# A hybrid decoder layer: the down projection of its FFN as two passes of Strassen's seven products

## The chip, the cores and the metric

One NeuronCore of a Trainium2 chip runs the whole program. The metric is the device time of one execution in microseconds (us), over several executions. One more execution was recorded by the profiler; its rows are shown below.

## What is computed

One layer in float32 on 512 tokens of width 1024. Three mixers (a conv module, a sparse attention, a Mamba-2 scan) come first. Behind them stands the FFN, which is all that the change touches (D_FF is 2816):

```python
h = rms_norm(x, norm_ffn_g[i])
f = causal_dwconv(h @ w_up[i], ffn_conv_w[i], ffn_conv_b[i])      # 512 x 5632, 3 taps
fa, fg = jnp.split(f, 2, axis=-1)
x = x + (jax.nn.silu(fg) * fa) @ w_down[i]                          # (512 x 2816) @ (2816 x 1024)
```

## The kernel before

Every large product is done in three matmuls: an operand a is split into a high part (a_hi, a copy rounded to the matmul's type, by ScalarE) and a rest (a_lo = a - a_hi, by VectorE), and `product` adds a_hi*b_hi, a_hi*b_lo and a_lo*b_hi in one PSUM bank. A matmul is 128x128 stationary by 128x512 moving.

Weights come in chunks of 1 MB (128 partitions x 2048 floats). A chunk is loaded by SyncE's queue (SP) into one of NSLOT = 2 slots of `w_raw`, in two transfers of 512 KB; ScalarE writes `w_hi`, VectorE `w_lo`; then SP may load the chunk after next into that slot (it waits for `w_lo_ready`), and TensorE may use the chunk. No scheduler is at work in this part: each engine's program is a list in the order of the code, and semaphores join them.

**The up stage.** There are NF = 22 chunks, UP0 to UP0+21; I call them up chunks 0 to 21. Each holds 128 columns of both halves of w_up, and gives two PSUM groups (v = 0, 1) of 24 matmuls. From up chunk 1 on, all engines run loops over rounds of two chunks (s = 0, 1). While TensorE works on a chunk, ScalarE makes `w_hi` of the next, then for each group `f` (the bank times the last tap, plus the bias), then `sg` = silu of the gate. VectorE makes `w_lo` of the next chunk, two more taps on `f` for each group (which frees the bank, semaphores `drained`), `gg` = f*sg, and, once ScalarE has made `g_hi` of it, `g_lo`.

**The down stage.** TensorE takes 11 chunks of w_down (256 rows each) against `g_hi` and `g_lo`. Each chunk is 48 matmuls: 4 blocks of tokens x 2 halves of the columns x 2 blocks of rows x 3. All eight banks accumulate through the whole stage (DOWN_BANK; the four banks of the up stage come last). At the end VectorE adds each bank to x2 into `y_out` (L1495), and SP stores it.

## Time and profile before

| | |
|---|---|
| time, median of 3 runs | 732.29 us (732.28 to 732.38) |
| time of the profiled execution | 732.33 us |
| its span from the first to the last instruction | 730.6 us |
| TensorE busy | 711.4 us, 97% of the span |
| VectorE, ScalarE, GpSimd busy | 459.6, 350.6, 141.9 us |
| granted TensorE clock | 1.00 throughout |
| moved by DMA | 69.48 MB, a mean of 95 GB/s |

The profile is a page of sums and a trace that can be asked for single instructions. Busy is the share of time in which an engine had an instruction at work. A matmul's recorded duration (389 ns) is longer than its share of the time, since matmuls are pipelined: the distance from one start to the next is what counts. A wait is put down to the engine whose signal came last.

### The profile page before, as it was taken

How to read it: one execution, taken by the hardware profiler on the slowest of the kernel's cores; microseconds unless marked ns; L12 is line 12 of the kernel's file. 1: busy time of each engine (PE TensorE's matmuls, PEld its weight loads, DVE VectorE, ACT ScalarE, POOL GpSimd, SP SyncE). 2: the span in 40 equal slices, each digit the busy share in tenths (PEclk: the TensorE clock that was granted, in tenths of full speed). 3: DMA queues.
4: the chain of work that ended last, by engine and by line, in shares of the span. 5: the costliest groups of instructions: out<-in, count | busy, mean ns of one | idle time of the engine just before them, and what ended most of it. 6: DMA issues, size and time to landing. Idle time of an engine off the chain costs nothing.

```text
span 730.6 us, 9609 instructions
## 1 busy us (share of the span) xinstructions
PE 711.4 (97%) x3468; PEld 572.1 (78%) x3468; DVE 459.6 (63%) x703; ACT 350.6 (48%) x532; POOL 141.9 (19%) x114
## 2 busy tenths in 40 slices
PE   4999999899999999999999999999999999999998
PEld 4776888667667788778798888888888888888886
DVE  5368989988998838777666655655656655221223
ACT  6354654989778585532654434434443443122120
POOL 2000569935555203143300000000000000000000
PEclk9999999999999999999999999999999999999999
DMA  9731314123031141212423343243243233322302
GB/s 247 231 116 59 116 59 115 59 79 95 12 103 43 52 195 60 87 58 59 116 58 84 89 115 92 81 115 100 72 115 108 64 115 115 116 66 107 116 1 115
DMA packets 78048, 69.48 MB, mean 95 GB/s; under 512 B 5815, under 2 KB 64535, under 8 KB 78015
## 3 DMA queue, kind: packets, MB, share of 16 engines
q1 hardware_dynamic: 77871, 68.51, 30.7%
q10 hardware_dynamic: 144, 0.52, 0.2%
q8 instruction: 21, 0.34, 0.2%
q14 instruction: 12, 0.10, 0.0%
HBM read 66.91 MB, written 2.12 MB: 94 GB/s over the span
## 4 chain that ended last, share of the span: by engine, by line
PE 86%; ACT 7%; DVE 4%; issue 2%; DMA 1%; POOL 0%; DVEq 0%; ACTq 0%
PE bank L1507 76%; PE bank L1513 3%; PE bank L1527 2%; ACT w_hi L857 1%; ACT tapped L1052 1%; PE bank L1715 1%; DVE u_acc L604 1%; PE bank L1771 1%; PE bank L1691 1%; DVE xbcT L1302 1%; PE bank L1666 1%; DMA x_in<-in_x 1%; ACT prob L975 1%; ACT dec L1022 0%; DVE prob L1281 0%
## 5 line engine op out<-in xcount | busy, mean ns | idle before, releaser
L1507 PE MATMUL bank<-h_hi,w_hi 128*128 128x512 f32 (+1 forms) x496 | 192.9, 389 | 0.0
L1507 PE MATMUL bank<-h_lo,w_hi 128*128 128x512 f32 (+1 forms) x496 | 189.9, 383 | 0.0
L1507 PE MATMUL bank<-h_hi,w_lo 128*128 128x512 f32 (+1 forms) x496 | 189.8, 383 | 0.0
L614 DVE TENSOR_TENSOR w_lo<-w_raw,w_hi 128x2048 fp32r<-128x2048 f32 x34 | 78.5, 2309 | 83.3 <-ACT w_hi L857 83.2
L1507 PEld LDWEIGHTS bank<-h_hi,w_hi 128*128 128x128 f32 x496 | 93.2, 188 | 25.4 <-issue 7.8
L1507 PEld LDWEIGHTS bank<-h_hi,w_lo 128*128 128x128 f32 x496 | 93.2, 188 | 18.6
L1507 PEld LDWEIGHTS bank<-h_lo,w_hi 128*128 128x128 f32 x496 | 93.3, 188 | 17.3
L857 ACT ACTIVATE w_hi<-w_raw 128x2048 fp32r<-128x2048 f32 x34 | 65.0, 1911 | 80.3 <-PE bank L1507 77.8
L783 POOL TENSOR_TENSOR u_acc<-tapped,u_acc 128x511 f32<-128x511 f32 (+29 forms) x60 | 90.1, 1502 | 46.1 <-ACT tapped L1052 43.0
L1468 DVE SCALAR_TENSOR_TENSOR f<-bank,prm,f 128x511 f32<-128x511 f32 x88 | 65.8, 748 | 51.3 <-ACT f L1102 44.9
L1102 ACT ACTIVATE f<-bank,prm 128x512 f32<-128x512 f32 x44 | 33.9, 770 | 95.3 <-PE bank L1507 95.3
L1507 PE MATMUL bank<-w_hi,g_hi 128*128 128x512 f32 x176 | 68.5, 389 | 0.0
L1507 PE MATMUL bank<-w_lo,g_hi 128*128 128x512 f32 x176 | 68.5, 389 | 0.0
L1507 PE MATMUL bank<-w_hi,g_lo 128*128 128x512 f32 x176 | 68.5, 389 | 0.0
L1460 DVE TENSOR_TENSOR w_lo<-w_raw,w_hi 128x2048 fp32r<-128x2048 f32 x22 | 50.4, 2292 | 23.1 <-ACT w_hi L1094 23.1
L604 DVE SCALAR_TENSOR_TENSOR u_acc<-u_in,prm,u_acc 128x511 f32<-128x511 f32 (+29 forms) x60 | 51.9, 877 | 0.8
L1507 PE MATMUL bank<-w_hi,h_hi 128*128 128x512 f32 x128 | 51.2, 400 | 0.0
L1052 ACT ACTIVATE tapped<-u_in,prm 128x511 f32<-128x511 f32 (+29 forms) x60 | 40.1, 703 | 21.4 <-POOL u_acc L783 15.5
L1507 PE MATMUL bank<-w_hi,h_lo 128*128 128x512 f32 x128 | 50.0, 390 | 0.0
L1507 PE MATMUL bank<-w_lo,h_hi 128*128 128x512 f32 x128 | 49.9, 390 | 0.0
L763 POOL TENSOR_TENSOR stats<-stats 128x1 f32<-128x1 f32 (+1 forms) x24 | 23.1, 967 | 103.3 <-DVE stats L1382 35.1
L1094 ACT ACTIVATE w_hi<-w_raw 128x2048 fp32r<-128x2048 f32 x22 | 41.8, 1902 | 0.0
(234 smaller groups left out, 1006.6 us busy)
## 6 DMA issues: line engine op xcount, KB each, us to landing
w_raw<-in_w_up SPq DMA_DIRECT2D x44, 512.0 KB, 4.7
w_raw<-in_w_in SPq DMA_DIRECT2D x34, 512.0 KB, 4.6
w_raw<-in_w_down SPq DMA_DIRECT2D x22, 512.0 KB, 3.9
w_raw<-in_w_out SPq DMA_DIRECT2D x12, 512.0 KB, 4.4
x_in<-in_x SPq DMA_DIRECT2D x4, 512.0 KB, 6.9
tbias<-distance_table SPq DMA_DIRECT2D x1, 2048.0 KB, 8.0
x<-in_x SPq DMA_DIRECT2D x4, 512.0 KB, 7.2
out_x<-y_out SPq DMA_DIRECT2D x8, 256.0 KB, 2.0
```

What stands on the lines that cost most here:

```text
L604: eng.scalar_tensor_tensor(out=u_acc[:, j, i:], in0=u_in[:, j, 0:SEQ - i], scalar=w, in1=u_acc[:, j, i:], op0=ALU.mult, op1=ALU.add).then_ ...
L614: eng.tensor_tensor(wlo[:, slot, cols], wraw[:, slot, cols], whi[:, slot, cols].bitcast(F32), ALU.subtract).then_inc(ready, 1)
L763: pool.tensor_tensor(out_, in_, half_neg[:, 0:n], ALU.pow).then_inc(ready, 1)
L783: pool.tensor_tensor(u_acc[:, j, i:], tapped[j][:, i % 4, 0:SEQ - i], u_acc[:, j, i:], ALU.add).then_inc(dw_taps[j], 1)
L857: act.activation(whi[:, c % NSLOT, :], wraw[:, c % NSLOT, :], ACT.Copy)\
L1052: act.activation(tapped[j][:, i % 4, 0:SEQ - i], u_in[:, j, 0:SEQ - i], ACT.Copy, scale=prm[:, c:c + 1]).then_inc(dwp_ready, 1)
L1094: act.activation(whi[:, c % NSLOT, :], wraw[:, c % NSLOT, :], ACT.Copy)\
L1102: act.activation(fbuf[:, 2 * s + v, :], bank[FFN_BANK[2 * s + v]][:, :], ACT.Identity, bias=prm[:, bass.ds(tile + R_FB, 1)], scale=prm[:, ...
L1460: dve.tensor_tensor(wlo[:, c % NSLOT, :], wraw[:, c % NSLOT, :], whi[:, c % NSLOT, :].bitcast(F32), ALU.subtract)\
L1468: ins = dve.scalar_tensor_tensor(out=fbuf[:, 2 * s + v, i:], in0=bank[FFN_BANK[2 * s + v]][:, 0:SEQ - i], scalar=prm[:, bass.ds(tile + (R_ ...
L1507: ins = pe.matmul(o, a, b, start=first and i == 0 and q == 0, stop=last and i == n - 1 and q == 2)
L1513: return pe.transpose(o, in_, ident[0:n, 0:n])
```

## The change

The product of the activations (512 x 2816) with w_down (2816 x 1024) is cut into 2 x 2 blocks of blocks: tokens in two halves of 256, rows of w_down in two halves of 1408 (11 tiles of 128; NP2 = 11), columns in two halves of 512. Strassen's method forms seven products of sums of such blocks in place of eight. They are done in two passes, since a product takes two banks: four products in the first pass (FIRST: m6, m2, m4, m1), three in the second (SECOND: m5, m3, m7). A pass runs over 11 tiles; the text calls one tile of a pass a pair, pairs 0 to 10 and 11 to 21. A pair is 4 x 2 x 3 = 24 matmuls in the first pass, 18 in the second.

What is new around it:
- **Weight sums.** In each round of the up stage VectorE forms five 128x512 sums of w_down's blocks (`weight_sums`). SP loads the blocks (1 MB, `load_blocks`) and stores the sums to memory (1.31 MB, `store_sums`); the down stage loads them back. These transfers stand between the loads of the up chunks in SP's queue.
- **Activation sums.** gg is kept whole (`g_raw`). For each pair VectorE forms sums of its blocks (`g_sum`), ScalarE and VectorE split them and one plain block into `g_parts`. Pairs 0 to 3 are prepared in rounds 1 to 4 of the up stage (`pair=True`), the others two pairs ahead in the down stage.
- **Slots.** The down stage has 4 raw slots, 3 of hi and lo, 5 of parts. Loads are 1 MB a pair in the first pass, 0.75 MB in the second.
- **Order.** The up chunks come in the order 0, 11, 1, 12, ... of w_up's tiles, so that both halves of a pair are ready together. In ScalarE's list `sg` now stands between the two `f` of a chunk. The first and the last round stand outside of the loops.
- **Outputs.** Products are added to x2 by VectorE, two or four 128x512 instructions in pairs 12 to 17 and ten behind the last product (`add_to`). ScalarE copies four banks to `kept` between the passes.
- GpSimd has nothing to do in this part, before as after.

The diff, cut to its core:

```diff
         RING[g] = (ring, n, first + n % count, n // count)
-DOWN_BANK = [7, 4, 5, 6] + FFN_BANK
+PAIR_BANK = [(7, 4), (5, 6), tuple(FFN_BANK[0:2]), tuple(FFN_BANK[2:4])]
...
     with ExitStack() as ctx:
...
-        y_out = at("y_out", [P, 8, 512], F32, ffn)
+        kept = at("kept", [P, 4, 512], F32, ffn)
+        draw = [wraw[:, DN0 % 2, :], at("down_raw1", [P, 2048], F32, mix0 + 76 * K)[:, :],
+                wraw[:, 1 - DN0 % 2, :], at("down_raw3", [P, 2048], F32, h0)[:, :]]
+        dhi = [whi[:, DN0 % 2, :], whi[:, 1 - DN0 % 2, :],
+               at("down_hi2", [P, 2048], F32R, h0 + 8 * K)[:, :]]
...
+        def width(p):
+            return 2048 if p < NP2 else 1536
...
+            def load_blocks(j):
+                sp.dma_start(blocks[:, 0:1024], w_down[bass.ds(j * P, P), :]).then_inc(s_stage, 16)
+                sp.dma_start(blocks[:, 1024:2048], w_down[bass.ds(j * P + NP2 * P, P), :])\
+                    .then_inc(s_stage, 16)
+            def store_sums(j):
+                sp.wait_ge(w_sum_ready, j * 5 + 5)
+                sp.dma_start(wsums[bass.ds(j * P, P), 0:1024], w_sum[:, :]).then_inc(s_sums, 16)
+                sp.dma_start(wsums[bass.ds(j * P, P), 1024:2560], blocks[:, 0:1536])\
+                    .then_inc(s_sums, 16)
+            sp.wait_ge(acc_step, STEP[("wo", "conv", 1, NT - 1)])
+            load_blocks(0)
+            store_sums(0)
+            with sp.Fori(0, NP2 - 1) as n:
...
+                    if s == 0:
+                        sp.wait_ge(s_sums, n * 32 + 32)
+                        load_blocks(n + 1)
+                    else:
+                        store_sums(n + 1)
+            sp.wait_ge(s_sums, 32 * NP2)
...
+                if p == 0:
+                    sp.wait_ge(w_lo_ready, DN0 - 1)
+                elif p == 2:
+                    sp.wait_ge(w_lo_ready, DN0)
+                elif p == 3:
+                    sp.wait_ge(acc_step, STEP0 + 2 * NF)
+                elif p >= NRAW:
+                    sp.wait_ge(w_lo_ready, DN0 + p - NRAW + 1)
+                j = p % NP2
+                r0, r1_ = P * j, P * (j + NP2)
+                dst, done = draw[p % NRAW], d_landed[p % NRAW]
+                if p < NP2:
+                    sp.dma_start(dst[:, 0:512], w_down[r0:r0 + P, 0:512]).then_inc(done, 16)
+                    sp.dma_start(dst[:, 512:2048], wsums[r0:r0 + P, 0:1536]).then_inc(done, 16)
+                else:
+                    sp.dma_start(dst[:, 0:1024], wsums[r0:r0 + P, 1536:2560]).then_inc(done, 16)
+                    sp.dma_start(dst[:, 1024:1536], w_down[r1_:r1_ + P, 512:1024]).then_inc(done, 16)
...
+            for p in range(ND - 2):
+                load_down(p)
...
-            with act.Fori(0, NF // 2) as n:
+            def up_two(n, pair=False, last=False):
...
-                        act.wait_ge(acc_step, n * 4 + STEP0)
+                    if last and s == 1:
+                        act.wait_ge(d_landed[0], 32)
                     else:
-                        act.wait_ge(acc_step, n * 4 + STEP0 + 2)
+                        act.wait_ge(w_landed[c % NSLOT], n * 32 + 32 * (c // NSLOT + 1))
+                    act.wait_ge(acc_step, n * 4 + (STEP0 + 2 * s))
...
                         act.wait_ge(acc_step, n * 4 + STEP0 + 2 * s + v + 1)
-                        tile = n * 2 + (s + (NF if v == 0 else 0))
+                        if last and (s, v) == (1, 1):
+                            down_hi(1)
...
-                    act.wait_ge(drained[FFN_BANK[2 * s]], n + (ROUND0[2 * s] + 1))
-                    act.activation(sg[:, s, :], fbuf[:, 2 * s, :], ACT.Silu).then_inc(sg_ready, 1)
-                    act.wait_ge(gg_ready, n * 2 + (s + 2))
-                    act.activation(ghi[:, bass.ds(n * 2 + s, 1), :],
-                                   gg[:, s:s + 1, :], ACT.Copy).then_inc(ghi_ready, 1)
-            for c in range(DN0 + 1, len(CHUNKS)):
-                split_hi(c)
+                        if v == 0:
+                            act.wait_ge(drained[FFN_BANK[2 * s]], n + (ROUND0[2 * s] + 1))
+                            act.activation(sg[:, s, :], fbuf[:, 2 * s, :], ACT.Silu)\
...
+                    if pair and s == 0:
+                        p = n + (-1)
+                        act.wait_ge(g_sum_ready, n * 2)
+                        hi = part[:, bass.ds(p, 1), 0, :]
+                        act.activation(hi[:, :, 0:768], gsum[0][:, :].unsqueeze(1), ACT.Copy)\
+                            .then_inc(ghi_ready, 1)
+                        act.activation(hi[:, :, 768:1024], g_raw[:, bass.ds(n + (NP2 - 1), 1), 256:512],
+                                       ACT.Copy).then_inc(ghi_ready, 1)
...
+            def down_hi(p):
+                act.wait_ge(d_landed[p % NRAW], 32 * (p // NRAW + 1))
+                if p in (1, 2):
+                    act.wait_ge(acc_step, STEP0 + 2 * NF)
+                else:
+                    act.wait_ge(pair_done, p - NHI + 1)
+                act.activation(dhi[p % NHI][:, 0:width(p)], draw[p % NRAW][:, 0:width(p)], ACT.Copy)\
+                    .then_inc(w_hi_ready, 1)
...
+            up_two(0)
+            with act.Fori(1, AHEAD + 1) as n:
+                up_two(n, pair=True)
+            with act.Fori(AHEAD + 1, NP2 - 1) as n:
+                up_two(n)
+            up_two(NP2 - 1, last=True)
+            for p in range(2, ND):
+                down_hi(p)
+                if AHEAD <= p + 2 < ND:
+                    parts_hi(p + 2)
+                if p == NP2 + 1:
+                    for n, b in enumerate(PAIR_BANK[1] + PAIR_BANK[2]):
+                        act.wait_ge(m_done, 2 + n + 1)
+                        act.activation(kept[:, n, :], bank[b][:, :], ACT.Copy).then_inc(m_kept, 1)
...
+            def weight_sums(j):
+                b11, b12, b21, b22 = (draw[1][:, 512 * k:512 * k + 512] for k in range(4))
+                dve.wait_ge(s_stage, j * 32 + 32)
+                dve.tensor_tensor(w_sum[:, 0:512], b11, b12, ALU.add).then_inc(w_sum_ready, 1)
+                dve.tensor_tensor(w_sum[:, 512:1024], b11, b21, ALU.subtract)\
+                    .then_inc(w_sum_ready, 1)
+                dve.tensor_tensor(b11, b11, b22, ALU.add).then_inc(w_sum_ready, 1)
+                dve.tensor_tensor(b12, b12, b22, ALU.subtract).then_inc(w_sum_ready, 1)
+                dve.tensor_tensor(b21, b21, b22, ALU.add).then_inc(w_sum_ready, 1)
...
+                    if first and s == 0:
+                        weight_sums(0)
+                    if s == 1 and not last:
+                        weight_sums(n + 1)
...
+                    if last and s == 1:
+                        down_lo(1)
...
+            parts_sum(AHEAD)
+            for p in range(2, ND):
+                if p == NP2 + 1:
+                    for t in range(2):
+                        dve.wait_ge(m_done, t + 1)
+                        add_to(2 + t, 1, bank[PAIR_BANK[0][t]][:, :], ALU.add)
+                down_lo(p)
+                if p + 2 < ND:
+                    parts_lo(p + 2)
+                if p + 3 < ND:
+                    parts_sum(p + 3)
...
+            for t in range(2):
+                dve.wait_ge(m_done, 8 + t + 1)
+                add_to(t, 0, bank[PAIR_BANK[0][t]][:, :], ALU.subtract)
...
+            def part_product(p, m, w_col, g_col, t, first, last):
+                g_hi, g_lo = parts_of(p)
+                q = slice(256 * g_col + P * t, 256 * g_col + P * t + P)
+                f = slice(512 * w_col, 512 * w_col + 512)
+                return product(bank[PAIR_BANK[m][t]][:, :],
+                               [(g_hi[:, q], g_lo[:, q], dhi[p % NHI][:, f], dlo[p % NHI][:, f])],
+                               first=first, last=last)
...
+            for p in range(NP2):
+                pair_ready(p)
+                for m, (_, w_col, g_col) in enumerate(FIRST):
+                    for t in range(2):
+                        if p == 0:
+                            b = PAIR_BANK[m][t]
+                            pe.wait_ge(drained[b], DRAINS[b] + (NP2 if b < 4 else 0))
+                        ins = part_product(p, m, w_col, g_col, t, p == 0, p == NP2 - 1)
+                        if p == NP2 - 1:
+                            ins.then_inc(m_done, 1)
+                        elif (m, t) == (3, 1):
+                            ins.then_inc(pair_done, 1)
...
+                for m, (_, w_col, g_col) in enumerate(SECOND):
+                    for t in range(2):
+                        if p == NP2:
+                            if m == 0:
+                                pe.wait_ge(x_added, t + 1)
+                            else:
+                                pe.wait_ge(m_kept, 2 * m - 1 + t)
+                        ins = part_product(p, m, w_col, g_col, t, p == NP2, False)
...
+            pair_ready(ND - 2)
+            pair_ready(ND - 1)
+            for m, (_, w_col, g_col) in enumerate(SECOND):
+                for t in range(2):
+                    for p in (ND - 2, ND - 1):
+                        ins = part_product(p, m, w_col, g_col, t, False, p == ND - 1)
+                    ins.then_inc(m_done, 1)
```

VectorE at the start of the up stage, in before (the loop's first lines; the names are tiles, `f` the taps, and a row with ISA only carries a wait):

```order
L1460 TENSOR_TENSOR w_lo<-w_raw,w_hi 128x2048 [waits w_hi_ready]
L1465 ISA
L1468 ISA [waits f_ready]
L1468 SCALAR_TENSOR_TENSOR f<-bank,prm,f 128x511
L1468 ISA [waits ftap_ready]
L1468 SCALAR_TENSOR_TENSOR f<-bank,prm,f 128x510
```

The same place in the changed kernel (down_raw_127 is the slot that holds the blocks of w_down):

```order
L1584 TENSOR_TENSOR w_lo<-w_raw,w_hi 128x2048 [waits w_hi_ready]
L1572 TENSOR_TENSOR w_sum<-down_raw_127 128x512 [waits down_blocks_landed]
L1573 TENSOR_TENSOR w_sum<-down_raw_127 128x512
L1575 TENSOR_TENSOR down_raw_127<-down_raw_127 128x512
L1576 TENSOR_TENSOR down_raw_127<-down_raw_127 128x512
L1577 TENSOR_TENSOR down_raw_127<-down_raw_127 128x512
L1609 SCALAR_TENSOR_TENSOR f<-bank,prm,f 128x511 [waits f_ready]
L1609 SCALAR_TENSOR_TENSOR f<-bank,prm,f 128x510 [waits ftap_ready]
```

Five sums have moved in between `w_lo` of up chunk 1 and the taps of up chunk 0. SP's queue from up chunk 1's load into the loop, in before:

```order
L640 DMA w_raw<-in_w_up 128x8x128
L718 UNCONDITIONAL_BRANCH
L718 ISA
L726 ISA [waits w_lo_ready]
L726 DMA w_raw<-in_w_up 128x8x128
```

and in the changed kernel:

```order
L665 DMA w_raw<-in_w_up 128x8x128
L742 DMA down_raw_127<-in_w_down 128x1024 [waits acc_step]
L743 DMA down_raw_127<-in_w_down 128x1024
L748 DMA weight_sums<-w_sum 128x1024 [waits w_sum_ready]
L749 DMA weight_sums<-down_raw_127 128x1536
L755 UNCONDITIONAL_BRANCH
L755 ISA
L763 ISA [waits w_lo_ready]
L763 DMA w_raw<-in_w_up 128x8x128
```

The load of up chunk 2 now stands behind the store of the first sums. VectorE at the end of the up stage, in before (its last chunk, then the down stage):

```order
L1468 SCALAR_TENSOR_TENSOR f<-bank,prm,f 128x510
L1478 REGISTER_ALU
L1480 REGISTER_ALU [waits sg_ready]
L1482 TENSOR_TENSOR gg<-f,sg 128x512 [waits glo_ready,drained1]
L1486 ISA [waits ghi_ready]
L1486 TENSOR_TENSOR g_lo<-gg,g_hi 128x512
L1455 REGISTER_ALU
L1455 COMPARE_AND_BRANCH
```

and in the changed kernel, where L1641 is `down_lo`, of pair 1 and then of pair 2:

```order
L1609 SCALAR_TENSOR_TENSOR f<-bank,prm,f 128x511 [waits f_ready]
L1609 SCALAR_TENSOR_TENSOR f<-bank,prm,f 128x510 [waits ftap_ready]
L1641 TENSOR_TENSOR w_lo<-down_raw_127,w_hi 128x2048 [waits w_hi_ready]
L1623 TENSOR_TENSOR g_raw<-f,sg 128x512 [waits drained1,sg_ready]
L1654 TENSOR_TENSOR g_sum_121<-g_raw 128x256 [waits glo_ready,gg_ready]
L1656 TENSOR_TENSOR g_sum_121<-g_raw 128x512
L1641 TENSOR_TENSOR down_lo_130<-w_raw,down_hi_129 128x2048 [waits w_hi_ready]
```

`w_lo` of pair 1 stands behind the last taps. ScalarE's part of it is the line `down_hi(1)` of the diff, which stands ahead of the last `f`.

## Rows read from the trace of the kernel before

**Rows 1.** The page: busy time of engines, and engines' shares of the final chain.

```profile
PE 711.4 (97%) x3468; PEld 572.1 (78%) x3468; DVE 459.6 (63%) x703; ACT 350.6 (48%) x532; POOL 141.9 (19%) x114
...
PE 86%; ACT 7%; DVE 4%; issue 2%; DMA 1%; POOL 0%; DVEq 0%; ACTq 0%
```

**Rows 2.** Windows, up and down stage: stretch, length, busy (count) by engine, clock, DMA.

```profile
core 0: us, PE busy (x) PEld busy (x) DVE busy (x) ACT busy (x) POOL busy (x), PEclk, DMA share, GB/s
372.00:607.00 235.00, 235.00 (x1067) 195.86 (x1066) 142.36 (x151) 95.81 (x109) 0.00 (x0) 1.00 0.34 94
607.00:727.30 120.30, 120.30 (x532) 99.39 (x530) 30.64 (x21) 20.98 (x13) 0.00 (x0) 1.00 0.26 91
```

**Rows 3.** The chain that ended last, from 480 us: start, length, what.

```profile
479.88 247.53 PE bank L1507 x1092
727.42 0.02 issue
727.44 0.69 DVE y_out L1495
```

**Rows 4.** Timeline of TensorE: start, duration; first matmuls of stretches, and the last.

```profile
379.05 0.40 PE L1507 MATMUL bank<-h_hi,w_hi 128*128 128x512 f32 x1
...
389.96 0.39 PE L1507 MATMUL bank<-h_hi,w_hi 128*128 128x512 f32 x1
...
607.56 0.39 PE L1507 MATMUL bank<-w_hi,g_hi 128*128 128x512 f32 x1
...
613.00 0.39 PE L1507 MATMUL bank<-w_hi,g_hi 128*128 128x512 f32 x1
...
727.01 0.39 PE L1507 MATMUL bank<-w_hi,g_lo 128*128 128x512 f32 x1
```

**Rows 5.** Timeline of VectorE at the start of the up stage.

```profile
369.82 2.48 DVE L1133 TENSOR_TENSOR h_lo<-bank,h_hi 128x512 fp32r<-128x512 f32 x4 [0.55 <-ACT h_hi L845]
374.63 2.29 DVE L1460 TENSOR_TENSOR w_lo<-w_raw,w_hi 128x2048 fp32r<-128x2048 f32 x1 [2.33 <-ACT w_hi L1094]
...
385.31 2.29 DVE L1460 TENSOR_TENSOR w_lo<-w_raw,w_hi 128x2048 fp32r<-128x2048 f32 x1 [0.99 <-ACT w_hi L1094]
387.51 1.64 DVE L1468 SCALAR_TENSOR_TENSOR f<-bank,prm,f 128x511 f32<-128x511 f32 x2
```

**Rows 6.** Timeline of ScalarE there.

```profile
379.40 0.78 ACT L1102 ACTIVATE f<-bank,prm 128x512 f32<-128x512 f32 x1 [2.10 <-PE bank L1507]
380.08 0.62 ACT L1109 ACTIVATE sg<-f 128x512 f32<-128x512 f32 x1
...
383.37 1.90 ACT L1094 ACTIVATE w_hi<-w_raw 128x2048 fp32r<-128x2048 f32 x1
```

**Rows 7.** Timeline of SP's queue: the load of up chunk 3, its issue time.

```profile
377.08 1.00 SPq L726 DMA_DIRECT2D w_raw<-in_w_up  x2
```

**Rows 8.** Transfers in 377 to 383 us: GB/s in 40 slices, landing of each half.

```profile
GB/s 0 0 0 0 0 0 0 24 61 85 119 225 307 321 321 328 307 256 335 338 331 338 341 328 338 324 311 311 290 294 283 246 150 58 21 0 0 0 0 0
...
w_raw<-in_w_up SPq DMA_DIRECT2D x2, 512.0 KB, 4.5
```

**Rows 9.** The same in 717.5 to 723.5 us, three stores; the page on stores.

```profile
GB/s 0 0 0 0 0 0 0 0 0 0 0 0 0 287 369 355 396 328 14 0 0 0 273 396 341 396 314 28 0 0 0 259 341 396 396 314 41 0 0 0
...
out_x<-y_out SPq DMA_DIRECT2D x8, 256.0 KB, 2.0
```

**Rows 10.** Timeline at the end of the up stage, ScalarE, then VectorE.

```profile
607.90 0.78 ACT L1102 ACTIVATE f<-bank,prm 128x512 f32<-128x512 f32 x1 [4.34 <-PE bank L1507]
608.59 0.62 ACT L1109 ACTIVATE sg<-f 128x512 f32<-128x512 f32 x1
...
608.83 1.64 DVE L1468 SCALAR_TENSOR_TENSOR f<-bank,prm,f 128x511 f32<-128x511 f32 x2 [2.05 <-ACT f L1102]
610.50 0.69 DVE L1482 TENSOR_TENSOR gg<-f,sg 128x512 f32<-128x512 f32 x1
```

**Rows 11.** Groups of instructions: count, busy us, mean ns, idle before.

```profile
L1507 PE MATMUL bank<-w_hi,g_hi 128*128 128x512 f32 x176 | 68.5, 389 | 0.0
...
L1460 DVE TENSOR_TENSOR w_lo<-w_raw,w_hi 128x2048 fp32r<-128x2048 f32 x22 | 50.4, 2292 | 23.1 <-ACT w_hi L1094 23.1
...
L1094 ACT ACTIVATE w_hi<-w_raw 128x2048 fp32r<-128x2048 f32 x22 | 41.8, 1902 | 0.0
...
L1482 DVE TENSOR_TENSOR gg<-f,sg 128x512 f32<-128x512 f32 x12 | 8.3, 692 | 0.4
L1111 ACT ACTIVATE g_hi<-gg 128x512 f32 x12 | 7.6, 632 | 25.6 <-DVE gg L1482 25.6
```

More of the change, by code:

```diff
@@ L51 @@
 UP0 = len(CHUNKS)
-CHUNKS += [("up", j) for j in range(NF)]
+NP2 = NF // 2
+CHUNKS += [("up", j // 2 + NP2 * (j % 2)) for j in range(NF)]
 DN0 = len(CHUNKS)
-CHUNKS += [("down", j) for j in range(NF // 2)]
+ND = 2 * NP2
+NRAW, NHI, NPART, AHEAD = 4, 3, 5, 4
 NSLOT = 2
@@ L343 @@
     STEP[("chunk", UP0 + j)] = STEP0 + 2 * (j + 1)
-for j in range(NF // 2):
-    STEP[("chunk", DN0 + j)] = STEP0 + 2 * NF + j + 1
 SQ2 = [s for s in PLAN if s[0] == "sq2"]
@@ L375, in build @@
     gdram = nc.dram_tensor("distance_table", (NH, NG), F32, kind="Internal").ap()
+    wsums = nc.dram_tensor("weight_sums", (NP2 * P, 2560), F32, kind="Internal").ap()
     with ExitStack() as ctx:
@@ L564, in build @@
                              "glo_ready"))
-        y_ready = sem("y_ready")
+        d_landed = [sem(f"down_landed{n}") for n in range(NRAW)]
+        w_sum_ready, g_sum_ready = sem("w_sum_ready"), sem("g_sum_ready")
+        s_stage, s_sums = sem("down_blocks_landed"), sem("weight_sums_stored")
+        pair_done, m_done, m_kept = sem("pair_done"), sem("m_done"), sem("m_kept")
+        x_added = sem("x_added")
         block = ctx.enter_context(nc.Block())
@@ L640, in load @@
                         sp.dma_start(dst[:, :, s], src).then_inc(done, 16)
-                elif what == "down":
-                    dst = slot.rearrange("p (k n) -> p k n", k=2)
-                    for k in range(2):
-                        r = P * (2 * i + k)
-                        sp.dma_start(dst[:, k], w_down[r:r + P, :]).then_inc(done, 16)
                 else:
@@ new lines, in store @@
+            def store(t, half):
+                f = slice(512 * half, 512 * half + 512)
+                sp.dma_start(out[P * t:P * t + P, f], x2[:, t, f]).then_inc(s_yout, 16)
+            for p in range(ND - 2):
+                load_down(p)
+            for n in range(2):
+                sp.wait_ge(x_added, 10 + n + 1)
+                store(2 + n, 0)
+            load_down(ND - 2)
+            load_down(ND - 1)
+            for n, (t, half) in enumerate(((0, 1), (1, 1), (2, 1), (3, 1), (0, 0), (1, 0))):
+                sp.wait_ge(x_added, 14 + 4 + n + 1)
+                store(t, half)
@@ L1454, in _, with up_two @@
             dve.sem_inc(glo_ready, 1)
-            with dve.Fori(0, NF // 2) as n:
+            def weight_sums(j):
[7 more added lines that the diff above has]
+                dve.tensor_tensor(b21, b21, b22, ALU.add).then_inc(w_sum_ready, 1)
+            def up_two(n, pair=False, last=False, first=False):
                 for s in range(2):
@@ L1483, in _ @@
                         .then_inc(gg_ready, 1)
[L1484 to L1497 removed]
+                    if pair and s == 1:
+                        dve.wait_ge(ghi_ready, n * 2)
+                        hi, lo = (part[:, bass.ds(n + (-1), 1), w, :] for w in (0, 1))
+                        dve.tensor_tensor(lo[:, :, 0:768], gsum[0][:, :].unsqueeze(1),
+                                          hi[:, :, 0:768].bitcast(F32), ALU.subtract)\
+                            .then_inc(glo_ready, 1)
+                        dve.tensor_tensor(lo[:, :, 768:1024],
+                                          g_raw[:, bass.ds(n + (NP2 - 1), 1), 256:512],
+                                          hi[:, :, 768:1024].bitcast(F32), ALU.subtract)\
+                            .then_inc(glo_ready, 1)
@@ new lines, in _, with add_to @@
+            added, n_added = {}, [0]
+            def add_to(t, half, term, op):
+                if (t, half) in added:
+                    dve.wait_ge(x_added, added[(t, half)])
+                n_added[0] += 1
+                added[(t, half)] = n_added[0]
+                c = x2[:, t, 512 * half:512 * half + 512]
+                dve.tensor_tensor(c, c, term, op).then_inc(x_added, 1)
+            up_two(0, first=True)
+            with dve.Fori(1, AHEAD + 1) as n:
+                up_two(n, pair=True)
@@ new lines, in _ @@
+            for t in range(2):
+                dve.wait_ge(m_done, 8 + t + 1)
+                add_to(t, 0, bank[PAIR_BANK[0][t]][:, :], ALU.subtract)
+            for t in range(2):
+                add_to(t, 1, bank[PAIR_BANK[0][t]][:, :], ALU.add)
+            for t in range(2):
+                dve.wait_ge(m_done, 10 + t + 1)
+                add_to(t, 1, bank[PAIR_BANK[1][t]][:, :], ALU.add)
+            for t in range(2):
+                add_to(2 + t, 1, bank[PAIR_BANK[1][t]][:, :], ALU.add)
@@ L1500, in _ @@
+            for t in range(2):
+                dve.wait_ge(m_done, 12 + t + 1)
+                add_to(t, 0, bank[PAIR_BANK[2][t]][:, :], ALU.add)
         @block.tensor
```

164 lines of the change are left out of this document (113 added, 51 removed).

## The prediction

> **What bounds the kernel now.** I read the page first: TensorE is busy for 97% of the span and holds 86% of the chain that ended last [rows 1]. Then the windows of the two stages that the change touches: in both TensorE is busy all the time at a granted clock of 1.00, while VectorE is busy for 142.4 of 235 us in the up stage and 30.6 of 120.3 us in the down stage [rows 2]. The chain from 480 us on is one piece of TensorE, 247.5 us long, with one VectorE add behind it [rows 3]. So a matmul less is time saved, and anything that makes TensorE wait is time lost. The timeline gives the price: from the down stage's first matmul at 607.56 to its last at 727.01 there are 527 steps, 0.2267 us each [rows 4]. In the up stage 48 matmuls take 389.96 - 379.05 = 10.91 us, the same rate. It did not matter whether 24 or 6 matmuls in a row went to one bank, so I price the new runs of 3 at the same 0.2267.
>
> **What it removes.** The down stage had 528 matmuls (3 x 176 [rows 11]). Now there are 11 x 24 + 11 x 18 = 462. 66 x 0.2267 = **15.0 us off**. All the rest of the sum is TensorE waiting.
>
> **Prices of the added work.** VectorE: 2048 columns take 2.29 us, 512 take 0.69 [rows 11], so 1.04 ns a column and 0.16 fixed; by that 256 take 0.43, 768 0.96, 1536 1.76. Queued instructions start sooner than that: the next one 2.20 us behind w_lo, and four of 512 in 2.48, thus 0.60 apart [rows 5]. So I charge each its duration less 0.08. ScalarE: 1.90 and 0.63 for 2048 and 512 [rows 11], so 256 take 0.42, 768 0.84; the next one starts 0.68 behind a start of 0.78 [rows 6].
>
> **First stall: up chunk 2.** The queue orders above show the cause: the sums come behind w_lo of up chunk 1, and SP issues their two stores before it issues the load of up chunk 2.
> - w_lo of up chunk 1 starts at 374.63 [rows 5]; the five sums are done at 374.63 + 2.20 + 4 x 0.61 + 0.69 = 380.0.
> - SP reacts 0.16 us after w_lo's end and takes 0.5 us for each transfer [rows 5, 7]: stores at 380.1 and 380.6, loads at 381.1 and 381.6.
> - Bytes begin 1.0 us behind an issue, and a load of 1.05 MB has landed 5.0 us behind its first issue (377.58 + 4.5) [rows 7, 8]; it runs at some 310 GB/s, a store at 350 to 396 [rows 8, 9]. If they go in turn, 1.31 MB of stores take until 381.1 + 3.5 = 384.6, the load until 388.1.
> - w_hi 1.90 and w_lo 2.29 follow: 392.4. TensorE wants the chunk at 389.96 [rows 4]: **2.4 us lost**. Before, w_lo ended at 387.60, 2.4 early.
>
> Bounds: if the stores did not hold up the load at all, it lands at 386.1 and 0.4 us is lost; if they ran at half the rate, 5.9. The rows are nearest to the middle. The Trainium skill, "DMA: Bandwidth & Descriptors", section "Anatomy of one DMA", charges 2.0 us fixed and the bytes at 436 GB/s; as an estimate by that page the 2.36 MB land 7.4 us behind 380.1, the stall is 1.8 and the time 0.6 lower. By it a 256 KB store takes 2.6 us, where the row has 2.0 [rows 9], so it fits only roughly.
>
> **Later rounds.** The same order holds, but weight_sums then run a chunk earlier against the load they delay, so a load has some 5 us to spare. What is tight there is a loop through VectorE and ScalarE, since f of v = 1 now stands behind sg, which waits for the taps. In rounds 1 to 4 (`pair`) I walk it. s = 0: w_lo 2.21, sums of g 0.35 + 0.61, taps 1.64, signal 0.15, sg 0.54, f 0.68, parts 0.76 + 0.34, w_hi and the step to w_lo 1.93: 9.2. s = 1: w_lo 2.21, five weight sums 3.05, taps 1.64, 0.15, sg 0.54, f with its signal 0.92, taps 1.64, gg 0.64, parts 0.88 + 0.35: 12.0. Together 21.2 of TensorE's 21.8 us, so they hide, but after the first stall both engines are late and w_lo of up chunk 3 comes only some 0.2 us ahead. I add **0.5 us** for what that lets through (0 to 1). From round 5 on the parts are gone and there is slack of 5 us.
>
> **Second stall: pair 1.** Before, the last f starts at 607.90, taps at 608.83, gg at 610.50 [rows 10]. Now down_hi(1) stands ahead of that f: 607.90 + 1.81 + 0.93 + 1.67 = 612.3, then w_lo of pair 1 until 614.6. TensorE is through pair 0's 24 matmuls at 613.00 [rows 4]: **1.6 us lost** (1.2 to 2). The bank that the last taps free is wanted at 607.56 + 21 x 0.2267 = 612.3, just when it is free.
>
> **The rest of the down stage.** First pass, a pair: VectorE w_lo 2.21, parts 1.23, sums 0.96 = 4.4 of TensorE's 5.44; ScalarE 2.9. Second pass: VectorE w_lo 1.68, parts 0.96, sums 0.70 = 3.3 of 4.08, but 4.56 with two adds, in pairs 13 to 17 (pair 12 has four, two of them early). It starts w_lo of pair 13 at 2.5 us into the pass (ScalarE may split only behind pair 11's first group); five steps of 4.56 and 1.8 bring w_lo of pair 18 to 27.1, and TensorE wants it at 7 x 4.08 = 28.6. It holds with 1.5 us to spare. Between the passes banks 7 and 4 are added within 3 us of pair 10's start, and the four copies to `kept` need 4 x 0.7 of ScalarE; both are ready before pair 11 and its later groups ask. Transfers: 1.05 MB in 5.44 us and 0.79 in 4.08 are 193 GB/s, of which the loads hide in four slots. Behind the last matmul all stays: VectorE's last add waits for the last group alone, then 0.69, and a store of 2.0 [rows 3, 9].
>
> **The sum** against the profiled execution: 732.33 - 15.0 + 2.4 + 0.5 + 1.6 = **721.8**. That execution is 0.04 us from the median of 732.29. A change of 0.2% is 1.5 us.
>
> **Rivals.**
> - *Each instruction holds its engine for its whole recorded time.* The rows have 0.08 less for plain queued ones, but the new ones carry waits and strides. The walk of a round becomes 9.8 + 12.8 = 22.6 against 21.8: 0.8 to 0.9 a round over four rounds, and 0.6 on the way in. The first stall is 2.8, the second 1.7, and w_lo of pair 18 comes at 2.5 + 5 x 5.12 + 1.8 = 29.9, 1.3 late: 732.33 - 15.0 + 2.8 + 0.6 + 3.4 + 1.7 + 1.3 = 727.1. The Trainium skill, "VectorE: DVE Perf Modes", section "The DRAIN you can't avoid", says that the next instruction does not start until the pipe has emptied, a distance from start to start. By that rule this rival is right; the trace speaks against it, with starts 0.60 apart at 0.69 [rows 5].
> - *Transfers bound the up stage: slower.* A round moves 2.10 + 1.05 + 1.31 = 4.46 MB in 21.8 us, 205 GB/s, where it was 94 [rows 2]. If loads and stores together ran below 194 GB/s, each of 11 rounds would take 1.2 us longer, and the 13.4 us that the second stall leaves are gone. At 190 GB/s it is 11 x 1.7 = 19: 738. Against it: 0.34 of the engines' time at 94 GB/s, 0.26 at 91 in the down stage's long rows [rows 2], which makes a share of 0.34 + 0.31 = 0.65, and peaks of 310 and 396 [rows 8, 9].
> - *Stores don't hold up the load*, and the loops keep pace: 732.33 - 15.0 + 0.4 + 1.6 = 719.3.
> - *Short runs on a bank cost something.* At 0.03 us for each of the 154 runs: 726.4. Rows 4 show no such cost between runs of 24 and 6.
>
> **Chances.** The forecast, 720.3 to 724.5, 0.56; whole recorded times, 725 to 729, 0.22; no delay by the stores 0.08; short runs 0.04; transfers bind 0.08; others 0.02. The range 719.2 to 728.0 keeps the forecast, most of the whole-times case and the others on the fast side, some 0.82. Faster by over 0.2% is all but the transfers case and part of the unnamed: 0.89; same 0.03; slower 0.08.
>
> **What would show it.** TensorE's starts stay 0.227 apart in both passes. Its idle time is one piece of some 2.4 us ahead of up chunk 2, released by w_lo, with w_hi held by the load, and one of 1.6 ahead of pair 1. The down stage takes about 106.4 us. The weight sums start 0.61 apart. Idle pieces that repeat every second chunk in rounds 1 to 4, with no load behind them, would speak for whole times; pieces in all rounds, with w_hi waiting for a landing, for transfers. I am wrong if TensorE waits in the second pass, for `x_added`, `m_kept` or w_lo of pairs 17 to 20.

## The result, and the profile after

The changed kernel takes **725.04 us** (median of 4 runs, 724.17 to 725.39) against 732.34 us (732.28 to 732.38) of the kernel before on the same chip: a ratio of 0.9899, interval 0.9882 to 0.9916, so 7.3 us faster. The forecast was 721.8 us, range 719.2 to 728.0. The sign and the range hold; the middle is 3.2 us off, and that is the part to learn from. The result also lies outside 720.3 to 724.5, to which the prediction gave 0.56: the range holds it only because it was drawn wide enough for a rival that did not come true. A second series of the same kernel gave 722.59 to 725.88 in four runs, and this spread has a cause of its own, below. Two disturbed executions, of 998.28 us (this kernel, second series, mean granted clock 0.658) and of 1795.68 us (the kernel with twice the stores), are left out.

The page of the changed kernel, with the rows that answer to [rows 1]:

```profile
PE 698.9 (97%) x3398; PEld 561.2 (78%) x3402; DVE 545.2 (75%) x851; ACT 380.6 (53%) x569; POOL 141.9 (20%) x114
...
PE 81%; ACT 8%; DVE 5%; issue 3%; DMA 2%; POOL 0%; SPq 0%; POOLq 0%; DVEq 0%; ACTq 0%
```

TensorE still holds the end, but with 81% of the chain where it had 86: ScalarE, VectorE and a transfer have got in. The windows, up stage and down stage, as in [rows 2]:

```profile
core 0: us, PE busy (x) PEld busy (x) DVE busy (x) ACT busy (x) POOL busy (x), PEclk, DMA share, GB/s
372.00:613.50 241.50, 237.82 (x1066) 197.63 (x1066) 168.20 (x201) 91.16 (x97) 0.00 (x0) 0.99 0.67 203
613.50:723.20 109.70, 105.41 (x464) 86.66 (x462) 90.78 (x120) 55.48 (x62) 0.00 (x0) 1.00 0.52 175
```

TensorE's busy time in the up stage is 3.7 us short of the window, and the granted clock is 0.99, not 1.00: two losses, in one place. The chain that ended last shows where; before it was one piece of TensorE from 480 us on [rows 3]:

```profile
381.53 7.61 DMA w_raw<-in_w_up
389.14 0.02 issue
389.17 1.92 ACT w_hi L1164
391.08 0.02 issue
391.11 2.30 DVE w_lo L1584
393.41 0.13 issue
393.54 220.33 PE bank L1747 x960
...
618.12 2.21 DVE w_lo L1641
620.33 0.04 issue
620.37 99.63 PE bank L1747 x438
720.00 0.02 issue
720.03 0.69 DVE x L1685
```

There are just two breaks, those that the prediction named: the load of up chunk 2 with its two conversions, and w_lo of pair 1. Behind 620.37 TensorE runs without a wait to the last matmul. The timeline of TensorE at the first break, to be held against [rows 4]:

```profile
389.48 0.39 PE L1747 MATMUL bank<-h_hi,w_lo 128*128 128x512 f32 x1
393.54 0.79 PE L1747 MATMUL bank<-h_hi,w_hi 128*128 128x512 f32 x1 [3.68 <-DVE w_lo L1584]
394.13 0.63 PE L1747 MATMUL bank<-h_lo,w_hi 128*128 128x512 f32 x1
394.56 0.63 PE L1747 MATMUL bank<-h_hi,w_lo 128*128 128x512 f32 x1
```

From 389.48 to 393.54 is 4.06 us, where 0.2267 is the step: **3.83 us lost**. Then comes something that the prediction did not have: the matmuls start 0.427 us apart, not 0.227. The windows behind the break show why:

```profile
389.50:393.54 4.04, 0.36 (x2) 0.01 (x1) 2.43 (x2) 2.24 (x2) 0.00 (x0) 0.80 1.10 338
393.54:398.80 5.26, 5.26 (x13) 4.15 (x14) 4.28 (x7) 0.91 (x2) 0.00 (x0) 0.51 0.48 162
398.80:430.00 31.20, 31.20 (x139) 25.85 (x138) 23.58 (x29) 13.45 (x16) 0.00 (x0) 1.00 0.87 257
```

After 3.8 us of idle TensorE the granted clock is 0.51, the 1.2 GHz level, for 5.3 us; then it is back at 2.4 GHz. It fell while TensorE was still idle: the window of the wait itself has a mean of 0.80. TensorE is busy for all of that window, so no wait and no share of busy time shows this loss, only the clock's column and the distance of the starts. Summed over the steps it is **2.5 us**. The second break, ahead of pair 1:

```profile
618.91 0.39 PE L1747 MATMUL bank<-w_hi,g_parts 128*128 128x512 f32 x1
620.37 0.51 PE L1747 MATMUL bank<-w_hi,g_parts 128*128 128x512 f32 x1 [1.08 <-DVE w_lo L1641]
620.71 0.40 PE L1747 MATMUL bank<-w_lo,g_parts 128*128 128x512 f32 x1
```

It costs 1.23 us and 0.11 in the step behind it: **1.3 us**. All together: 732.33 - 15.0 + 3.8 + 2.5 + 1.3 = 724.9; the profiled execution took 724.93.

Why up chunk 2 was late by more than forecast stands in SP's queue and the transfers of 379 to 391 us (GB/s in slices of 0.3 us, then each issue's size and time to landing):

```profile
379.70 0.34 SPq L748 DMA_DIRECT2D weight_sums<-w_sum  x1
380.08 0.43 SPq L749 DMA_DIRECT2D weight_sums<-down_raw  x1
380.89 1.94 SPq L763 DMA_DIRECT2D w_raw<-in_w_up  x2
```

```profile
GB/s 0 0 0 0 0 382 410 396 437 451 328 328 328 328 164 164 184 164 266 79 280 350 346 346 336 301 287 294 294 285 326 369 341 369 423 410 423 437 396 335
...
w_raw<-in_w_up SPq DMA_DIRECT2D x4, 512.0 KB, 7.1
...
weight_sums<-down_raw SPq DMA_DIRECT2D x1, 768.0 KB, 5.5
```

The stores start at 380 to 450 GB/s, above the 350 to 396 that the prediction had, but once SP issues the load behind them (from 380.89 on) the rate falls to 328 and then 164. Their bytes run from 380.6 to some 385.0, so 1.31 MB took 4.4 us (300 GB/s), not 3.5, and the larger store has landed 5.5 us behind its issue, at 385.6. From 385.0 to the load's landing at 389.14 it is another 4.1 us, where the prediction had 3.5. The two halves of the load took SP 1.94 us to issue, not 1.0 as in [rows 7].

### The profile page after: what moved, and what is told of

It is laid out like the page before. It is cut to its first block, busy times and chain, and to the rows that moved or that the text cites. A ratio compares the mean times of both kernels' runs of the same rounds, so it can differ in the third digit from the quotient of the medians.

```text
span 723.2 us, 9804 instructions
## 1 busy us (share of the span) xinstructions
PE 698.9 (97%) x3398; PEld 561.2 (78%) x3402; DVE 545.2 (75%) x851; ACT 380.6 (53%) x569; POOL 141.9 (20%) x114
## 4 chain that ended last, share of the span: by engine, by line
PE 81%; ACT 8%; DVE 5%; issue 3%; DMA 2%; POOL 0%; SPq 0%; POOLq 0%; DVEq 0%; ACTq 0%
PE bank L1747 70%; PE bank L1753 3%; PE bank L1767 2%; ACT w_hi L927 1%; ACT tapped L1122 1%; PE bank L1955 1%; DMA w_raw<-in_w_up 1%; DVE u_acc L621 1%; PE bank L2011 1%; PE bank L1931 1%; DVE xbcT L1415 1%; PE bank L1906 1%; ACT prob L1045 1%; DMA x_in<-in_x 1%; DVE w_lo L1584 1%
## 5 line engine op out<-in xcount | busy, mean ns | idle before, releaser
L639 DVE TENSOR_TENSOR w_lo<-w_raw,w_hi 128x2048 fp32r<-128x2048 f32 x24 | 55.6, 2316 | 9.1 <-ACT w_hi L927 9.0
L1584 DVE TENSOR_TENSOR w_lo<-w_raw,w_hi 128x2048 fp32r<-128x2048 f32 x22 | 50.3, 2286 | 9.7 <-ACT w_hi L1164 9.7
L1747 PE MATMUL bank<-w_hi,g_parts 128*128 128x512 f32 x168 | 54.1, 390 | 1.1 <-DVE w_lo L1641 1.1
L1179 ACT ACTIVATE sg<-f 128x512 f32<-128x512 f32 x22 | 13.9, 632 | 74.1 <-DVE f L1609 74.1
L927 ACT ACTIVATE w_hi<-w_raw 128x2048 fp32r<-128x2048 f32 x24 | 45.8, 1910 | 3.9 <-DMA w_raw<-in_w_in 2.5
L1164 ACT ACTIVATE w_hi<-w_raw 128x2048 fp32r<-128x2048 f32 x22 | 41.9, 1906 | 6.7 <-DMA w_raw<-in_w_up 6.7
L1747 PEld LDWEIGHTS bank<-w_hi,g_parts 128*128 128x128 f32 x168 | 31.6, 188 | 8.0 <-DVE w_lo L1641 1.5
```

Source lines behind the costliest of these rows:

```text
L639: eng.tensor_tensor(wlo[:, slot, cols], wraw[:, slot, cols], whi[:, slot, cols].bitcast(F32), ALU.subtract).then_inc(ready, 1)
L927: act.activation(whi[:, c % NSLOT, :], wraw[:, c % NSLOT, :], ACT.Copy)\
L1164: act.activation(whi[:, c % NSLOT, :], wraw[:, c % NSLOT, :], ACT.Copy)\
L1584: dve.tensor_tensor(wlo[:, c % NSLOT, :], wraw[:, c % NSLOT, :], whi[:, c % NSLOT, :].bitcast(F32), ALU.subtract)\
L1747: ins = pe.matmul(o, a, b, start=first and i == 0 and q == 0, stop=last and i == n - 1 and q == 2)
```

## The experiments

All are edits of the changed kernel, 4 or 5 runs each; the kernel before took 732.23 to 732.36 us (medians) beside them. The diffs are cut to what matters.

### The load ahead of the stores

```diff
 load_blocks(0)
+load_up(0, 0)        # up chunk 2
 store_sums(0)
-load_up(0, 0)        # it stood here, as the loop's first load
 ...
```

> Changed against the changed kernel: in SP's queue the load of up chunk 2 stands ahead of the first two stores of weight sums; everything else is as it was. My theory (the stores ahead of the load, their wait for the sums and their bytes, make the first stall of 3.83 us, and that idle makes TensorE run at the lower clock for the next 12 matmuls, some 2.4 us): both go, 725.0 - 3.8 - 2.4 = 718.8 us, with the granted clock at 1.00 all through the start of the up stage. Rival 1, the lower clock has another cause (the matmuls on new banks, the transfers' load): the stall goes and the slow matmuls stay, 721.2. Rival 2, the stall is made by the sums on VectorE (w_lo(2) late) and not by the queue: 725.0, no change.

Measured: **718.86 us** (718.55 to 718.97), mean clock 0.999 to 1.000 in each run. TensorE has no gap from 365 to 480 us, and the windows behind the place show the clock at 1.00:

```profile
391.00:399.00 8.00, 8.00 (x37) 6.64 (x36) 6.46 (x9) 3.88 (x4) 0.00 (x0) 1.00 0.88 255
```

Stall and slow matmuls went together, 6.2 us by one line that moved. Both rivals fall: it is the queue's order, not the sums on VectorE, and the lower clock goes with the idle (the next kernel tests that alone). This kernel also shows what the same two stores do when no load is issued behind them. They are issued at 380.06 and 380.46, and the transfers of 378 to 392 us (slices of 0.35 us) read:

```profile
GB/s 0 0 0 0 0 0 0 0 293 410 398 386 521 334 456 386 404 158 0 0 0 59 94 152 246 351 480 398 374 386 434 290 319 350 338 309 298 293 290 290
...
weight_sums<-down_raw SPq DMA_DIRECT2D x1, 768.0 KB, 4.2
```

Their 1.31 MB take 3.5 us, from 380.8 to 384.3, which is the prediction's figure; with the load issued behind them they took 4.4 in the changed kernel, and the rate falls in the same way in the profiles of the three other kernels that kept this order (both with filler, and down_hi(1) later).

### Filler for TensorE

```diff
+pe.wait_ge(drained[7], DRAINS[7])
+for i in range(16):
+    pe.matmul(bank[7][:, :], hhi[:, i % KD, 0:P], hlo[:, i % KD, :], start=True, stop=True)
 with pe.Fori(0, NF // 2 - 1) as n:      # up chunk 2 and on
```

> Changed against the changed kernel: TensorE runs 16 more matmuls of 512 columns into the free bank 7 (their result is not used) before it waits for up chunk 2; they fill the 3.8 us of the first stall. The queues are as they were, so up chunk 2 is late by as much. My theory (the lower clock behind the stall comes from TensorE's idle): up chunk 2 still starts near 393.5 us in the trace, but with the granted clock at 1.00 and starts 0.227 apart: 725.0 - 2.4 = 722.6 us. Rival, the lower clock does not come from the idle: the 12 slow matmuls stay, 725.0 or up to 0.3 more.

Measured: **722.86 us** (722.81 to 722.98), mean clock 1.000 in all four. Up chunk 2 is as late as before, yet its matmuls run at full speed:

```profile
393.30:399.00 5.70, 5.68 (x25) 4.37 (x25) 4.98 (x8) 0.65 (x2) 0.00 (x0) 1.00 0.55 167
```

25 matmuls in 5.7 us, where the changed kernel had 13 in 5.3. So the slow matmuls are not due to new banks or to the transfers: work that nobody needs gave back 2.2 us because it kept TensorE from being idle. (Some executions keep the clock without filler, 2 of 12 as shown below; with it all four did.)

### Half the filler

The same with 8 matmuls.

> The changed kernel with 8 filler matmuls in place of the 16 of the second kernel: TensorE is idle ahead of up chunk 2 for 2.0 us in place of 3.8 (or of 0.2). This is near the stall of 2.4 us that the prediction gave. Runs so far: after 3.8 us idle mean clocks of 0.995 to 0.998 in 10 of 12 executions, 1.000 in two; after 2.6 us (the kernel with doubled stores) 1.000 in three and 0.998 in two. If a wait of 2.0 us already costs the clock at times: 722.6 with a clock of 1.000 in some executions and 723.6 to 725 with 0.995 to 0.998 in others. If it is too short for that: 722.6 to 722.9 and 1.000 in all.

Measured: median 723.46, but in two groups: 722.53 and 722.58 with a mean clock of 0.999, 724.33 and 724.53 with 0.997. The profile is of one of the latter; TensorE lost 2.0 us in the wait (its start at 393.65, the last of the filler at 391.44, less a step of 0.23), and the clock fell all the same:

```profile
393.60:397.60 4.00, 3.95 (x10) 3.12 (x11) 3.96 (x7) 0.00 (x0) 0.00 (x0) 0.57 0.33 85
```

So a stall of the 2.4 us that the prediction gave can be expected to bring this loss too in some executions; just that length was not run, but 2.0 here and 2.6 below were.

### The changed kernel again

> The changed kernel itself once more, to see whether its clock falls behind the first stall in each execution. The runs so far: median 725.0, 724.2 to 725.4; with down_hi(1) moved one profile had the whole stall of 3.83 us and the granted clock at 1.00 (721.37), three others took 722.8 to 723.75 with a mean clock of 0.995 to 0.998. If the fall is by execution: a time between 722.6 (no fall, clock 1.000) and 725.3 (clock 0.995), lower where the mean clock is higher. If each execution of this kernel has it: all within 0.3 of 725.0.

Measured: 725.88, 725.56 and 725.68 us with a mean clock of 0.995, and **722.59 with 1.000**. So the loss is by execution: it is there in most, and where it isn't, the same program is 3 us faster.

### down_hi(1) later

```diff
-if last and (s, v) == (1, 1):
-    down_hi(1)
 act.activation(fbuf[:, 2 * s + v, :], ...)
+if last and (s, v) == (1, 1):
+    down_hi(1)
```

> Changed against the changed kernel: ScalarE's conversion down_hi(1), 1.9 us, stands behind the last f of the up stage and no longer ahead of it. My theory (down_hi(1) ahead of the last f makes the second stall, 1.3 us in two parts ahead of pair 1): the stall goes, 725.0 - 1.3 = 723.7 us. Rival, w_lo of pair 1 then becomes late by the same, since down_hi(1) itself ends 1.8 us later and VectorE's subtraction of 2.3 us follows it: ahead of pair 1 TensorE waits as long or longer, 725.0 to 726.0.

Measured: 722.80, 722.99 and 723.75 us with mean clocks of 0.995 to 0.998, and 721.37 with 1.000. TensorE has no gap from 480 us to its end, so the rival falls: w_lo of pair 1 is no later than TensorE wants it. Compared at like clocks the gain is 1.2 us at 1.000 (722.59 to 721.37) and 1.4 to 1.9 at 0.995 (725.16 and 725.6 to 723.75). The profile is of the execution of 721.37 us, and it is the best witness on the clock: the whole first stall stands in it, and the matmuls behind it start 0.23 apart.

```profile
389.79 0.39 PE L1747 MATMUL bank<-h_hi,w_lo 128*128 128x512 f32 x1
393.85 0.49 PE L1747 MATMUL bank<-h_hi,w_hi 128*128 128x512 f32 x1 [3.67 <-DVE w_lo L1584]
394.18 0.39 PE L1747 MATMUL bank<-h_lo,w_hi 128*128 128x512 f32 x1
394.40 0.39 PE L1747 MATMUL bank<-h_hi,w_lo 128*128 128x512 f32 x1
```

### Both edits

> The edits of the first and the third kernel together: load of up chunk 2 ahead of the first stores, down_hi(1) behind the last f. If both theories hold and the two stalls are independent: 725.0 - 3.8 - 2.4 - 1.3 = 717.5 us, 15.0 - 0.2 below the 732.3 of the kernel before, so no stall is left between the two kernels. If one of them falls, what its single kernel shows, added: 718.8 with the first alone, 723.7 with the third alone.

Measured: **717.21 us** (717.17 to 717.54), ratio 0.9796 (0.9783 to 0.9809), and 717.39 (717.17 to 717.67) in a second series. No gap of TensorE from 365 us on. 732.25 - 15.0 = 717.2: with the waits gone the 66 matmuls are the whole difference between the kernels. It beats the changed kernel by 7.8 us. Against the kernel with the load first alone, also at 0.999 to 1.000, it gains 1.65 us; the second stall, with the step behind it, is 1.34 of that in the trace.

### Narrow stores first

The first round's stores carry 8 columns each; the rest follows behind the load, so all is stored.

```diff
+sp.wait_ge(w_sum_ready, 5)
+store_part(0, 8, 0, 8)
+load_up(0, 0)                   # up chunk 2
+store_part(8, 1024, 8, 1536)
+sp.wait_ge(s_sums, 64)
+load_blocks(1)
+load_up(0, 1)                   # up chunk 3
```

> Changed against the changed kernel, in the first round alone: the two stores ahead of up chunk 2's load carry only 8 columns of each tile, and two stores with the other columns follow behind the load (so all is stored). SP still waits for all five sums before the load, but the load's bytes no longer stand behind the stores' 1.31 MB. If the stores' bytes make the first stall (my theory): the load lands near 385.7 instead of 389.1, the stall shrinks from 3.8 to 0 to 0.5 us and the clock stays up, 718.8 to 719.4 us. Rival, the wait for the sums and the two issues make most of it (SP reaches the load only at 380.9): the stall stays above 2 us, 721 to 725.

Measured: **725.02 us** (724.95 to 726.30). The total says that my theory fell, the timeline says where it held. The stall ahead of up chunk 2 shrank from 3.83 to 1.07 us: 2.8 of it were the stores' bytes, and 1.1 is the late place in the queue. But a new one of 3.26 us stands ahead of up chunk 3, with the lower clock behind it. SP's queue, then TensorE's timeline:

```profile
380.77 1.06 SPq L763 DMA_DIRECT2D w_raw<-in_w_up  x2
381.87 1.24 SPq L753 DMA_DIRECT2D weight_sums<-w_sum  x1
383.15 0.43 SPq L754 DMA_DIRECT2D weight_sums<-down_raw  x1
389.69 0.34 SPq L742 DMA_DIRECT2D down_raw<-in_w_down  x1
390.07 0.43 SPq L743 DMA_DIRECT2D down_raw<-in_w_down  x1
390.55 1.06 SPq L763 DMA_DIRECT2D w_raw<-in_w_up  x2
```

```profile
390.99 0.49 PE L1759 MATMUL bank<-h_hi,w_hi 128*128 128x512 f32 x1 [0.92 <-DVE w_lo L1596]
...
405.26 0.49 PE L1759 MATMUL bank<-h_hi,w_hi 128*128 128x512 f32 x1 [3.10 <-DVE w_lo L1596]
```

VectorE and ScalarE ahead of the new stall:

```profile
394.68 0.69 DVE L1584 TENSOR_TENSOR w_sum<-down_raw 128x512 f32<-128x512 f32 x1 [3.83 <-DMA down_raw<-in_w_down]
...
400.47 1.90 ACT L1176 ACTIVATE w_hi<-w_raw 128x2048 fp32r<-128x2048 f32 x1
```

SP waits for the landing of the stores before it may load new blocks, and this time they landed late: the blocks are loaded from 389.69 on, where the changed kernel had 385.75. VectorE was idle for 3.83 us until they had landed at 394.7. Its five sums stand ahead of the taps of up chunk 1, these ahead of ScalarE's sg and f, and f ahead of w_hi and w_lo of up chunk 3, so all of them came late, w_lo from 402.85 to 405.14. The load of up chunk 3 itself was late too (issued at 390.55, where the changed kernel had 386.91) but held nothing up: it landed near 397.5, and w_hi began only at 400.47, right behind f.

In this execution the granted clock was still 1.00 in the wait (402.0 to 405.2) and fell some 1 us behind it: 0.64 in 405.2 to 410.0, eight steps of 0.427, 1.6 us. It adds up to 717.2 + 1.2 (up chunk 2) + 3.4 (up chunk 3) + 1.6 + 1.3 (pair 1) = 724.7. I had asked what the stores hold up, and not what waits for the stores.

### Twice the stores

Both edits, both up loads of a round ahead of the stores, and each store made twice.

> The kernel with both edits, with two more things: in every round both loads stand ahead of the stores, and all weight sums are stored twice, the second time into a tensor of its own that nobody reads (14.4 MB more; 5.77 MB in a round of 21.8 us instead of 4.46). If transfers are no limit of the up stage in this size (DMA share 0.66 at 202 GB/s in the later rounds, so some 0.86 at 262 GB/s): 717.2 us as with both edits, TensorE's starts 0.227 apart. Rival, the mixed traffic holds 250 GB/s at most (the first rounds' rows show 235 to 274): 23.1 us for a round, 10 rounds at 1.3 us, 730 us.

Measured: 720.11, 720.17 and 720.21 us with a mean clock of 1.000, 721.78 and 722.16 with 0.998. More than the 717.2 expected, and far from the rival's 730. The one wait is again ahead of up chunk 3, 2.59 us and 0.10 behind it, for the same reason as in the kernel above: the stores landed at 387.8, the blocks at 392.95, and VectorE was idle for 5.57 us ahead of its sums. It accounts for 717.2 + 2.7 = 719.9; the last 0.2 to 0.3 us are not placed. In the later rounds, where the question was put, TensorE never waits at 265 GB/s, and the DMA share is 0.78, not the 0.86 expected:

```profile
430.00:608.00 178.00, 178.00 (x787) 147.50 (x786) 127.53 (x151) 67.71 (x71) 0.00 (x0) 1.00 0.78 265
```

### More work for VectorE in the second pass

Both edits, and in pairs 13 to 17 one more addition of 1024 columns into a tile that nobody reads.

> The kernel with both edits, and one more 1024-column addition on VectorE (into a tile that nobody reads by then; 2 x 0.60 = 1.2 us) in each of the pairs 13 to 17 of the second pass: 6.0 us. In the kernel with both edits VectorE has no idle from pair 13 on and ended w_lo of pair 18 at 693.86, TensorE wanted it at 695.8. My theory (this margin of 1.9 us is all that covers VectorE there): TensorE waits 6.0 - 1.9 = 4.1 us in all ahead of pairs 16 to 18, 717.2 + 4.1 = 721.3 us, or up to 2.4 more where its clock falls after the waits. Rival, VectorE has more slack than the one row shows: 717.2 to 719.

Measured: **721.27 us** (721.02 to 721.28), 3.9 above the kernel with both edits beside it. TensorE loses 0.8, 1.5 and 1.5 us ahead of pairs 16, 17 and 18 (0.1 of each in the step behind the wait), each time for w_lo; the one ahead of pair 17:

```profile
693.90 0.50 PE L1758 MATMUL bank<-down_hi,g_parts 128*128 128x512 f32 x1 [1.24 <-DVE down_lo L1647]
```

The addition has 1.14 us from its start to the next one's (689.76 to 690.89), so 5.7 us were added, and 5.7 - 3.9 leaves a cover of 1.8 us. The clock stayed at 0.999 to 1.000 in all five runs.

## Where the prediction was right, and where wrong

- **15.0 us off**: right. With the waits gone the kernel is 15.0 us faster than before. The starts are 0.227 apart in runs of 3 as in runs of 24, so the rival of the short runs falls.
- **First stall, 2.4 us**: right in place, cause and releaser (w_lo, with w_hi held by the load), too small in size; it is 3.8, inside its bounds. The step that was off is "If they go in turn, 1.31 MB of stores take until 381.1 + 3.5 = 384.6, the load until 388.1"; the load landed at 389.14. Two terms of it were too small. The stores' rate came from rows of stores with no load issued behind them [rows 9]: their bytes took 4.4 us and not 3.5, and since they began 0.5 earlier they ended 0.4 later, near 385.0. The load was charged 3.5 us, its bytes at the full rate, though the rows have 4.0 from its first byte to its landing (5.0 behind its first issue, less the 1.0 until bytes begin [rows 7, 8]); here it is 4.1. That is 1.0 us; 0.13 is the signal from VectorE to TensorE, which I had left out, and some 0.3 that this execution wants the chunk earlier (389.7, not 389.96). (My sum of 388.1, 1.90 and 2.29 is 392.3, not 392.4.) The estimate by the Trainium skill, "DMA: Bandwidth & Descriptors", "Anatomy of one DMA", had all bytes landed 7.4 us behind the first store's issue; the trace disagrees, with 9.4 (379.70 to 389.14). That section fits its figures to transfers that GpSimd issues, and these are SP's, which the prediction passed over.
- **The cost behind the stall**: missing. The sum had a stall as so many microseconds and no more. Idle TensorE lost its clock, 2.5 us in the profiled execution. This is the term that failed, put at nothing without a reason, and most of the error, 2.5 of 3.1 us: 721.8 + 1.4 (first stall) + 2.5 (clock) - 0.5 - 0.3 = 724.9. The start of the up stage had the clock at 1.00 in the rows of before because nothing there waited, so it said nothing on what a wait would do.
- **0.5 us in later rounds**: wrong, nothing is lost. The loop of 21.2 in 21.8 us fits, late start or not.
- **Second stall, 1.6 us**: right, 1.3. The edit that removes it removes that stall and no more.
- **The rest of the down stage hides**: right. TensorE never waits in the second pass; w_lo of pair 18 is there with 1.95 us to spare (forecast 1.5), and the kernel with more additions shows that this is all the cover there is. The down stage takes 719.60 - 613.69 + 0.23 = 106.1 us, forecast 106.4.

```profile
699.82 1.74 DVE L1641 TENSOR_TENSOR w_lo<-w_raw,w_hi 128x1536 fp32r<-128x1536 f32 x1
```

```profile
703.51 0.39 PE L1747 MATMUL bank<-w_hi,g_parts 128*128 128x512 f32 x1
```

- **The rival of whole recorded times, 727.1 with 0.22**: its number lies 2 us from the result, its band of 725 to 729 holds the result, and it is still wrong: no loss stands where it put them. The five weight sums last 0.69 and start 0.60 apart, and rounds 1 to 4 have no wait:

```profile
376.58 0.69 DVE L1572 TENSOR_TENSOR w_sum<-down_raw 128x512 f32<-128x512 f32 x1
377.18 0.68 DVE L1573 TENSOR_TENSOR w_sum<-down_raw 128x512 f32<-128x512 f32 x1
```

  With the rule of the Trainium skill, "VectorE: DVE Perf Modes", "The DRAIN you can't avoid", taken as a distance from start to start, the trace disagrees, for these instructions as for those of before [rows 5]. The same paragraph says that a next instruction which is not held starts earlier; the rival had left that out, and the starts 0.60 apart at 0.69 agree with it.
- **The rival that transfers bind**: the changed kernel moves 203 GB/s in the up stage, as worked out (205), at a DMA share of 0.67 (0.65). With stores doubled it holds 265 with TensorE never waiting, far above the deciding 194.

**Open:** why the same wait costs the clock in one execution and not in the next, and whether the stores' rate falls because of the load's packets or of its issue. On the second the runs show only that the same two stores take 4.4 us with a load issued behind them and 3.5 without; load packets and issue were not tried apart.

## What to carry to other kernels

A store that stands ahead of a load in one queue delays it twice, by the wait for its data and by its bytes, and whatever waits for the store's landing is next in the line, here another load and, through VectorE's list, the taps and the next conversion; put the load that TensorE needs first, and then ask what stands behind the wait for the landing. Price a stall of TensorE not only by its length: look at the granted clock behind it, and reckon with 1.4 to 3.3 us on top of it. Here that came in 14 of 16 executions with a wait of 3.3 to 3.8 us, in 4 of 9 with one of 2.0 to 2.6, and in none of 5 with waits of 0.7 to 1.4. When a total comes out near a rival's number, read the place of the loss before the rival is believed.
